# A hybrid decoder step on one core: the mixer in one pass of 576 tokens, and in two token groups with u tiles between the steps of the second

## The chip, the cores and the metric

One Trainium2 chip, one of its cores. The metric is the device time of one execution in microseconds; the kernel was run three times, and one execution more was taken with the hardware profiler.

## The reference

There are 576 tokens of width 1024: 512 of a prompt and 64 of a sample group (8 sequences of 8). Cut to what matters, for both groups:

```python
xn = rms_norm(x, norm1_g)
q, k, v, glu = _project(xn, w_in, q_g, k_g)          # 8 heads of 64, 2 kv heads; glu = val * sigmoid(gate), 512 channels
a = sliding-window attention with sinks (prompt: blocks of 128; sample: cached keys and values, then the new ones)
c = silu(layer_norm(causal depthwise conv of glu, width 31)) @ conv_pw_w
h = x + concat(rms_norm(a), rms_norm(c)) @ w_out
y = h + _peer(rms_norm(h))                            # PEER: 8 heads, top 16 of 128 x 128 experts per token
# _peer: scores of two half-keys, the 16 best of each, the 16 best sums, gate = softmax of those;
#        out = sum over the picks of gelu(u[i] . xn) * gate * v[i], with 16384 experts of width 1024
```

## The kernel before, in words

Five token tiles (`TILES`): tiles 0 to 2 are the 384 dense tokens (`DT`), tile 3 (`TA`, 128 tokens of the prompt) and tile 4 (`TB`, the 64 sample tokens) are the 192 gathered ones (`GT`). Activations lie transposed, channels on the partitions, tokens in the free dimension.

The *mixer* works on all 576 tokens at a time. TensorE multiplies weight blocks out of a ring of four (`wring`, loaded by `load_block` on SP's queue when the block four places earlier has been used) with `xn` (`gemm`, L523): K, four Q, V, then for each of four channel groups the GLU value and gate. Attention goes through eight *units* (token tile, kv head): scores (L589), softmax on VectorE and ScalarE (`softmax_max`, L833, `softmax_div`), transposes (L600), values (L611). There is one buffer of probabilities, so units follow one another. VectorE does the depthwise convolution of three of the four channel groups between the halves of the softmaxes, as chains of 31 dependent taps, each tap one instruction of 512 columns (prompt) and one of 64 (sample) (`conv_taps` at the file's end, L1454; which quarter goes where is `CONV_AT`); TensorE does the fourth with diagonal matrices (L578, L579). Then come the sample's scores, transposes and values (L624 to L643), the means and roots of the norms (`means` L535, `root` L805 on ScalarE, `rstd` L1078 on VectorE), the pointwise product `pw`, the output product in two halves (`woa` of attention, `wob` of convolution), and the second norm (L1223).

*PEER.* The two halves of the experts' work are done in two ways. For the 192 gathered tokens, routing comes first (`key_ranks("a")`, `picks` of TA and TB); then GpSimd gathers for each of 128 picks one row of `u` and one of `v` per token (384 "rows" of 512 KB in all, L1056, ring of 8), and VectorE multiplies or accumulates them (`row`, L1348, L1352). For the 384 dense tokens all 16384 experts are computed: 128 *u tiles* (`dense_u`, L710, 24 matmuls each), each split into a high and a low part by ScalarE (`high`, L915) and VectorE (`low`, L1233), with a Gelu out of PSUM (L941) that SP stores to DRAM; and 128 *v tiles* (L782, 18 matmuls each). Between the two stands the *gate stage*: 64 batches of six tokens, in which VectorE builds two one-hot matrices (`onehots`, L1395), ScalarE scales one (`apply_gates`, L996), TensorE multiplies them (L760), ScalarE copies the result to `Gs` (L1010), all double-buffered, and SP stores it.

The order on every engine is written out by hand, and a few constants say which u tile or row goes where: the u tiles 0 to 16 (`U_TOP` = 17) run beside the picks of TA and TB, 16 beside the ranking of the dense tokens (`key_ranks("b")`), 36 beside their picks, 54 are spread over the 64 gate batches by `u_at` (L62 to L64) and five come after. Of the rows, 66 come before the gate stage, 152 are spread over its batches by `batch_rows` (`V_ROW0`), and the rest over the v tiles by `v_rows`. `EXP_AFTER`, `KEYS_AFTER` and `ROWS_AFTER` name the u tile behind which ScalarE does a piece of the routing. No u tile starts before the keys of the gathered tokens are ranked. In the gate stage TensorE's order is this:

```python
for b in range(NBAT):
    pe.wait_ge(s_ab, 2 * b + 2)      # one-hots of batch b, VectorE
    pe.wait_ge(s_ag, b + 1)          # scaled, ScalarE
    if b >= 2:
        pe.wait_ge(s_gev, b - 1)     # copied out, ScalarE
    # six products, L760
    for n in range(u_at(b), u_at(b + 1)):
        dense_u(n)
```

and ScalarE's is: copy batch b (L1010), scale batch b + 1 (L996), then the Gelu and `high` of the batch's u tiles.

Of the kernel before, what the change touches and what calls it, by code (L numbers as in the profile page):

```python
# [58 lines left out]
U_TOP = 17  # L59
# [13 lines left out]
V_ROW0 = B_ROW0 + 152  # L73
# [13 lines left out]
ROWS_AFTER = {2: TA, 4: TB}  # L87
EXP_AFTER = {5: TA, 13: TB, 39: 0, 51: 1, 63: 2}
KEYS_AFTER = {8: TB, 33: 0, 45: 1, 57: 2}
# [21 lines left out]
BLOCKS += ["woa0", "woa1", "woa2", "pw0", "pw1"] + [f"woa{_m}" for _m in range(3, DC)] + [f"wob{_m}" for _m in range(DC)]  # L111
NMIX = len(BLOCKS)
ROW_WO = BLOCKS.index("woa0") + 2
# [3 lines left out]
def block_row(n):  # L117

    name = BLOCKS[n]
    if name[:2] == "wo":  # L120
        return ROW_WO + int(name[3:])
    if name[:2] == "pw":
        return ROW_WO - 2 + int(name[2:])
    return n if n < NMIX else ROW_WO + DC + (n - NMIX) % NM


def block_use(n):

    name = BLOCKS[n]
    if name[:3] == "val":  # L130
        return f"glu{2 * int(name[3:])}"
    if name[:4] == "gate":
        return f"glu{2 * int(name[4:]) + 1}"
    return {"pw0": "pw1", "pw1": "pw3"}.get(name, name)


CONV_AT = [0, 0, 0, 1, 2, 3, 4, 5, 6, 7, 8, 9, 10, 11, 12, 12, 12]
# [6 lines left out]
def psum_plan():  # L144

    plan = [("ms1", 3), ("K", 0), ("Q0", 1), ("Kn", 3), ("Q1", 2), ("Q0n", 3), ("Q2", 0), ("Q1n", 3), ("Q3", 1),
            ("Q2n", 3), ("V", 2), ("Q3n", 3)]
    for u in range(8):
        plan += [(f"S{u}", 2)] + ([(f"glu{2 * u}", 0)] if u < CC else []) + [(f"PT{u}", 3)]
        plan += ([(f"glu{2 * u + 1}", 1)] if u < CC else []) + [(f"O{u}", 2)]  # L150
    plan += [("taps", 0)]
    plan += [("SS", 2), ("PTS", 3), ("OS", 2), ("msA", 3), ("mean", 0), ("woa0", 2), ("var", 1)]
    plan += [("woa1", 3), ("woa2", 2), ("pw0", 0), ("pw1", 1), ("pw2", 3), ("pw3", 0), ("woa3", 2), ("msC", 1)]
    plan += [("woa4", 3), ("woa5", 0), ("woa6", 2), ("woa7", 3)]
    plan += [(f"wob{m}", m % 3) for m in range(DC)]
    plan += [("ms2", 3)]
# [5 lines left out]
    plan += [(f"xt{TA}", 0), (f"xt{TB}", 0)]  # L162
    for m in range(NM):
        plan += [(f"wqb{m}", m % 2), (f"scb{m}", 2)]
    plan += [(f"tr{t}", t % 2) for t in range(DTI)] + [(f"ht{TA}", 1), (f"ht{TB}", 0)]
    return plan


def hymba_peer(nc, xT_d, wblk_d, cols_d, maskp_d, masks_d, ident_d, ckT_d, cv_d, state_d, keysT_d, u_d, v_d, uT_d,
               gm_d, y_d, pk_d, pv_d, pc_d, sk_d, sv_d, sc_d):  # L170
    use = {}
    uses = [0] * 4
    for name, pair in psum_plan():
        uses[pair] += 1
        use[name] = (pair, uses[pair])

    with ExitStack() as ctx:
# [32 lines left out]
        idx = sb("idx", [P, 2, NPICK], I32)  # L210
        hu = sb("hu", [P, 2, NPICK])
# [3 lines left out]
        with ExitStack() as mixer:  # L215
# [4 lines left out]
            AT = mb("AT", [P, CC, T])  # L220
            cacc = mb("cacc", [P, CC, T])
            qT = mb("qT", [P, CC, T])
            kT = mb("kT", [P, T])
            vtok = mb("vtok", [P, 5, P])
            sq = mb("sq", [P, 2, T])
            Pb = mb("Pb", [P, 1024])
            PTb = mb("PTb", [P, 1024])
            sg = mb("sg", [P, 2, T])
            qS = mb("qS", [P, NDB * GQ * DS])
            maskp = mb("maskp_sb", [P, 2 * WIN])  # L230
            masks = mb("masks_sb", [P, 4, WIN + NS])
            ckT = mb("ckT", [P, NDB, WIN])
            cv = mb("cv", [P, NDB, P])
            gpad = mb("gpad", [P, CC, PAD + SEQ])
            spad = mb("spad", [P, CC, NDB, PAD + DS])
            taps = mb("taps", [P, TAPS, P])
            on1024 = mb("on1024", [P, P])
            on512 = mb("on512", [P, P])
            onblk = mb("onblk", [P, P])
            rs = mb("rs", [P, T])  # L240
            st = mb("st", [P, 8, 8])

        xh = sb("xh", [P, DC, DT], F32R)
        xl = sb("xl", [P, DC, DT], F32R)
        xtok = sb("xtok", [P, 2, D])
# [3 lines left out]
        raw = sb("raw", [P, RAWS, D])  # L249
        hi = sb("hi", [P, 2, D], F32R)  # L250
        lo = sb("lo", [P, 2, D], F32R)
        ring = sb("ring", [P, SLOTS, D])
        gest = sb("gest", [P, 2, 2 * DT])
# [32 lines left out]
        R = [sem(f"psum_ready{i}") for i in range(4)]  # L286
        F = [sem(f"psum_free{i}") for i in range(4)]
# [16 lines left out]
        s_conv_d = sem("conv_by_dve")  # L304
# [61 lines left out]
        def _(sp):  # L366
# [16 lines left out]
            def load_block(n):  # L383
# [3 lines left out]
                if BLOCKS[n][:2] == "wo":  # L387
# [34 lines left out]
            for n in range(NMIX + RING):  # L422
# [10 lines left out]
                if BLOCKS[n] == "woa0":  # L433
                    small_outputs()
                load_block(n)

            sp.wait_ge(s_xn2, DC)
            sp.wait_ge(s_o2, 16 * 15)
            for m in range(NM):
                if m < RAWS:  # L440
                    load_raw(m)
                load_block(NMIX + RING + m)
            for n in range(U_TOP):
                after_u(n)
# [58 lines left out]
        def _(pe):  # L503
            nblk = [0]

            def take(name):
                pair, n = use[name]
                if n > 1:
                    pe.wait_ge(F[pair], n - 1)
                return ps[pair], R[pair]  # L510

# [16 lines left out]

            def means(name, ones, src, n, made):

                out, ready = take(name)
                for k in range(n):
                    pe.wait_ge(made, k + 1)
                    for a in range(2):
                        mm = nc.tensor.matmul(out[:, a * 512:a * 512 + HALF], ones[:, :],  # L535
                                              src(k)[:, a * HALF:(a + 1) * HALF], start=(k == 0), stop=(k == n - 1))
                mm.then_inc(ready, 1)
# [28 lines left out]
            def conv_taps(i):  # L566
# [8 lines left out]
                pair, _ = use["taps"]  # L575
                for j in range(TAPS_AT[i], TAPS_AT[i + 1]):
                    ends = dict(start=(j == 0), stop=(j == TAPS - 1))
                    nc.tensor.matmul(ps[pair][:, 0:SEQ], taps[:, j, :], gpad[:, c, j:j + SEQ], **ends)  # L578
                    mm = nc.tensor.matmul(ps[pair][:, SEQ:T], taps[:, j, :], spad[:, c, :, j:j + DS], **ends)  # L579
                if i == 7:  # L580
                    mm.then_inc(R[pair], 1)

            for u in range(8):
# [8 lines left out]
                if u < CC:  # L592
                    gemm(f"glu{2 * u}", xn)
                else:
                    conv_taps(2 * (u - CC))
# [7 lines left out]
                if u < CC:  # L603
                    gemm(f"glu{2 * u + 1}", xn)
                else:
                    conv_taps(2 * (u - CC) + 1)
# [8 lines left out]

            pe.wait_ge(s_cache, 48)
            out, ready = take("SS")
            for b in range(NDB):
                for g in range(NKV):
                    grp, slot = b // 2, (b % 2) * 2 + g  # L620
                    rows = slice(g * HD, (g + 1) * HD)
                    o = out[slot * 32:slot * 32 + 32, (grp // 2) * 512 + (grp % 2) * 192:]
                    q = qS[rows, b * 32:(b + 1) * 32]
                    nc.tensor.matmul(o[:, 0:WIN], q, ckT[rows, b, :], start=True, stop=True)  # L624
                    mm = nc.tensor.matmul(o[:, WIN:WIN + NS], q, kT[rows, SEQ:T], start=True, stop=True)
            mm.then_inc(ready, 1)
            pe.wait_ge(s_p, 9)
            out, ready = take("PTS")
            for grp in range(4):
# [900 lines left out]
```

## Time and profile before

| | us |
|---|---|
| median of three runs | 1857.13 (1852.23 to 1859.45) |
| profiled execution, own time | 1858.78 |
| its span, first to last instruction | 1857.0 |
| TensorE matmul busy | 1669.9 (90%) |
| VectorE busy | 1433.3 (77%) |
| ScalarE busy | 762.1 (41%) |
| GpSimd busy | 540.2 (29%) |
| mean granted TensorE clock | 0.951 of full |

Busy times overlap between engines, and a busy matmul is not a matmul at its peak, so the shares alone don't name a bound. The kernel has stages with different limits, and the rows below are read by stage. Columns of groups of instructions are: line, engine, operation, what it writes and reads, partitions and elements, count, then busy us, mean ns of one, then the engine's idle time just before them and what ended it.

### The profile page before, as it was taken

The page shows a single profiled execution, that of the slowest core. Times are in us where ns is not written, and L with a number is a line of the kernel's source. Part 1 is how long each engine was busy: PE and PEld are TensorE (multiplying, and loading weights), DVE is VectorE, ACT ScalarE, POOL GpSimd, SP SyncE. Part 2 cuts the span into 40 slices and gives each one's busy share as a digit, 9 for nine tenths or more (in the row PEclk, how much of TensorE's full clock was granted, in tenths as well). Part 3 has the DMA queues.
Part 4 walks back from the last instruction along what each step waited for, and adds up shares of the span by engine and source line. Part 5 has one row for each costly group of instructions (what it writes and reads, how often), then busy time and mean ns, then how long its engine had stood idle before and what let it go on. Part 6 is the DMA issues. An engine that isn't in the chain of part 4 may idle for free.

```text
span 1857.0 us, 23142 instructions
## 1 busy us (share of the span) xinstructions
PE 1669.9 (90%) x8361; PEld 1449.5 (78%) x8361; DVE 1433.3 (77%) x2657; ACT 762.1 (41%) x1274; POOL 540.2 (29%) x395
## 2 busy tenths in 40 slices
PE   7888668989699998999789998999999999999997
PEld 5766446769697777999789898999877877877876
DVE  3466854238777999777899999995978888988876
ACT  3222112112352222444688887884333333333332
POOL 0000000000012333111366566662334433344330
PEclk9998887999799999999899999999999999999999
DMA  6110500125275787777699999999999999999985
GB/s 191 46 46 3 63 1 18 52 77 189 86 255 188 287 276 234 240 230 239 232 393 382 402 385 397 388 381 397 383 343 374 376 349 376 386 375 368 373 316 186
DMA packets 164360, 477.45 MB, mean 257 GB/s; under 512 B 28063, under 2 KB 61535, under 8 KB 162071
## 3 DMA queue, kind: packets, MB, share of 16 engines
q1 hardware_dynamic: 108951, 274.63, 42.6%
q0 software_dynamic: 55296, 201.35, 28.6%
q8 instruction: 67, 1.10, 0.2%
q14 instruction: 46, 0.38, 0.1%
HBM read 420.93 MB, written 54.42 MB: 256 GB/s over the span
## 4 chain that ended last, share of the span: by engine, by line
PE 60%; DVE 29%; issue 5%; ACT 3%; DMA 2%; SPq 0%; DVEq 0%; ACTq 0%
PE ps L782 24%; PE ps L710 17%; PE ps L523 9%; DVE ring L1348 6%; DVE lo L1233 3%; PE ps L760 3%; DVE cacc L1454 2%; DVE gA L1395 2%; DVE tsi L1245 2%; DVE tsi L1248 2%; DVE gB L1395 2%; PE ps L535 2%; DVE sm L1246 2%; DVE acc L1352 2%; DVE tsv L1247 1%
## 5 line engine op out<-in xcount | busy, mean ns | idle before, releaser
L1056 POOL DMA_INDIRECT ring<-in_u,idx x192 | 272.0, 1417 | 909.4 <-DVE ijg L1328 523.9
L1233 DVE TENSOR_TENSOR lo<-raw,hi 128x1024 fp32r<-128x1024 f32 x256 | 313.1, 1223 | 143.8 <-ACT hi L915 141.0
L915 ACT ACTIVATE hi<-raw 128x1024 fp32r<-128x1024 f32 x256 | 270.4, 1056 | 324.3 <-PE ps L782 324.3
L710 PE MATMUL ps<-xh,hi 128*128 128x384 f32 x1024 | 356.9, 349 | 27.2 <-DVE lo L1233 27.2
L1056 POOL DMA_INDIRECT ring<-in_v,idx x192 | 266.7, 1389 | 368.6 <-DVE acc L1352 354.7
L710 PE MATMUL ps<-xl,hi 128*128 128x384 f32 x1024 | 348.5, 340 | 0.0
L710 PE MATMUL ps<-xh,lo 128*128 128x384 f32 x1024 | 347.9, 340 | 0.0
L782 PE MATMUL ps<-hi,ah 128*128 128x512 f32 x768 | 239.9, 394 | 23.0 <-DVE al L1425 22.8
L1352 DVE SCALAR_TENSOR_TENSOR acc<-ring,hu,acc 128x1024 f32<-128x1024 f32 x192 | 245.5, 1279 | 1.6
L782 PE MATMUL ps<-hi,al 128*128 128x512 f32 x768 | 239.7, 394 | 0.0
L782 PE MATMUL ps<-lo,ah 128*128 128x512 f32 x768 | 239.1, 393 | 0.0
L1348 DVE CUSTOM_DVE_ANT_0 ring<-ring,xtok 128x1024 f32<-128x1024 f32 x192 | 226.4, 1218 | 0.3 <-DVE hu L1348 0.3
L710 PEld LDWEIGHTS ps<-xh,hi 128*128 128x128 f32 x1024 | 198.2, 194 | 29.3 <-issue 15.5
L710 PEld LDWEIGHTS ps<-xl,hi 128*128 128x128 f32 x1024 | 197.8, 193 | 0.0
L710 PEld LDWEIGHTS ps<-xh,lo 128*128 128x128 f32 x1024 | 197.0, 192 | 0.0
L782 PEld LDWEIGHTS ps<-hi,ah 128*128 128x128 f32 x768 | 145.5, 190 | 56.6 <-DVE lo L1233 23.5
L782 PEld LDWEIGHTS ps<-hi,al 128*128 128x128 f32 x768 | 146.0, 190 | 30.7
L782 PEld LDWEIGHTS ps<-lo,ah 128*128 128x128 f32 x768 | 145.9, 190 | 30.7
L941 ACT ACTIVATE gest<-ps 128x384 f32<-128x384 f32 x128 | 62.8, 491 | 248.6 <-PE ps L710 237.0
L1010 ACT ACTIVATE Gs<-ps 128x768 f32<-128x768 f32 x64 | 133.5, 2086 | 28.4 <-PE ps L760 28.4
L760 PE MATMUL ps<-gB,gA 128*128 128x128 f32 x768 | 106.1, 292 | 42.7 <-issue 26.3
L680 PE MATMUL ps<-xn,wring 128*128 128x192 f32 (+1 forms) x512 | 133.6, 416 | 5.6 <-DVE xn L1223 5.6
(176 smaller groups left out, 1972.7 us busy)
## 6 DMA issues: line engine op xcount, KB each, us to landing
raw<-in_uT SPq DMA_DIRECT2D x128, 512.0 KB, 5.9
raw<-in_v SPq DMA_DIRECT2D x128, 512.0 KB, 6.2
wring<-in_wblk SPq DMA_DIRECT2D x48, 512.0 KB, 3.5
gelu_matrix<-gest SPq DMA_DIRECT2D x64, 384.0 KB, 7.4
gate_matrix<-Gs SPq DMA_DIRECT2D x16, 1536.0 KB, 8.8
Gl<-gate_matrix SPq DMA_DIRECT2D x128, 192.0 KB, 6.6
gel<-gelu_matrix SPq DMA_DIRECT2D x128, 192.0 KB, 5.7
wring<-in_wblk SPq DMA_DIRECT2D x16, 256.0 KB, 2.5
```

The lines of the kernel that those rows point to most:

```text
L523: mm = nc.tensor.matmul(out[:, a * 512:a * 512 + HALF], w, rhs[:, k, a * HALF:(a + 1) * HALF], start=(k == 0), stop=(k == kc - 1))
L680: mm = nc.tensor.matmul(out[:, 0:w], wring[:, n % RING, k * P:(k + 1) * P], xn[:, k, t0:t0 + w], start=(k == 0), stop=(k == DC - 1))
L710: mm = nc.tensor.matmul(out, a[:, n % 2, w], b[:, c, :], start=(c == 0 and k == 0), stop=(c == DC - 1 and k == 2))
L760: mm = nc.tensor.matmul(ps[b % 2][:, c:c + NKEY], A[:, b % 2, t, :], B[:, b % 2, t, :], start=True, stop=True)
L782: mm = nc.tensor.matmul(ps[t][:, h * 512:(h + 1) * 512], a[:, n % 2, w], b[:, n % 2, h * 512:(h + 1) * 512], start=False, stop=(n == NKEY ...
L915: nc.scalar.activation(hi[:, s % 2, :], raw[:, s % RAWS, :], ACT.Copy).then_inc(s_hi, 1)
L1010: nc.scalar.activation(dst, src, ACT.Copy).then_inc(s_gev, 1)
L1056: pool.indirect_dma_start(ring[:, r % SLOTS, :], None, table, bass.IndirectOffsetOnAxis(idx[:, t, c:c + 1], 0)).then_inc(g_in[r % SLOTS], 16)
L1233: nc.vector.tensor_tensor(lo[:, s % 2, :], raw[:, s % RAWS, :], hi[:, s % 2, :].bitcast(F32), ALU.subtract).then_inc(s_lo, 1)
L1348: nc.vector.tensor_tensor_reduce(got, got, xtok[:, t, :], 1.0, 0.0, ALU.mult, ALU.add, hu[:, t, c:c + 1]).then_inc(g_used, 1)
L1352: nc.vector.scalar_tensor_tensor(out=acc[:, t, :], in0=got, scalar=hu[:, t, c:c + 1], in1=acc[:, t, :], op0=ALU.mult, op1=ALU.add).then_in ...
L1395: nc.vector.tensor_tensor(dst[:, b % 2], iota.unsqueeze(1).broadcast_to([P, BATCH, NKEY]), kT3[:, half, tok:tok + BATCH].unsqueeze(2).broa ...
```

## The change

The attention units and the channel means, norms, pointwise and output products are done for the 384 dense tokens first. The 192 gathered tokens go afterwards, in buffers of their own (`mgb`, `ATb`, `caccb`, `rsb`), with units 6 and 7, the sample's attention and the same chain of norms and products at 192 columns (one full output product `wo` in place of `woa` and `wob`; the pointwise and output blocks are loaded a second time). Between their steps TensorE runs u tiles 0 to 11 (`U_MIX` = 12), with `step` on ScalarE, `low` on VectorE and `after_u` on SP. All later due numbers are raised by 12, so that 42 u tiles are left for the gate batches; `V_ROW0` goes from 152 to 140 rows behind `B_ROW0`. The convolution on VectorE becomes `conv_a` (384 columns, all of it in units 1 to 3) and `conv_b` (128 and 64 columns, 12 quarters from unit 4 to unit 6). PSUM is handed out by banks of 512 columns instead of pairs of banks, and the buffers used only by the late part lie where `xtok`, `acc` and the row ring come later. Q, K, V and the GLU products stay as they are.

```diff
-U_TOP = 17
+U_MIX = 12
+U_TOP = U_MIX + 17
...
-V_ROW0 = B_ROW0 + 152
+V_ROW0 = B_ROW0 + 140
...
-CONV_AT = [0, 0, 0, 1, 2, 3, 4, 5, 6, 7, 8, 9, 10, 11, 12, 12, 12]
+CONV_AT = [0, 0, 0, 2, 4, 6, 8, 10, 12, 12, 12, 12, 12]
...
# SP
+                if BLOCKS[n] == "woa4":
+                    for s in range(RAWS):
+                        load_raw(s)
                 load_block(n)
-            sp.wait_ge(s_xn2, DC)
+            for n in range(8):
+                after_u(n)
...
# TensorE
+            unit_scores(4)
+            unit_scores(5)
+            conv_taps(0)
+            conv_taps(1)
+            unit_transposes(4)
+            conv_taps(2)
+            conv_taps(3)
+            unit_values(4)
+            conv_taps(4)
+            conv_taps(5)
+            unit_transposes(5)
+            conv_taps(6)
+            conv_taps(7)
+            unit_values(5)
...
+            dense_u(0)
+            dense_u(1)
+            unit_transposes(6)
+            unit_scores(7)
+            dense_u(2)
+            unit_values(6)
+            dense_u(3)
+            unit_transposes(7)
+            sample_scores()
+            dense_u(4)
+            unit_values(7)
+            pe.wait_ge(s_conv_b, CC)
+            group_means("meanb", lambda k: caccb[:, k, :], CC)
+            dense_u(5)
+            sample_transposes()
+            dense_u(6)
+            group_means("varb", conv_b, CC, s_sqc, base=CC)
+            sample_values()
+            dense_u(7)
+            group_means("msAb", lambda k: mgb[:, k, :], CC, s_sqa, base=CC)
+            for m in range(CC):
+                group_gemm(f"pwb{m}", ...)
+            dense_u(8)
+            group_means("msCb", conv_b, CC, s_sqcr, base=CC)
+            dense_u(9)
+            for m in range(DC):
+                group_gemm(f"wo{m}", ...)
+                if m >= 2:
+                    square_mean("ms2b", m - 2, DC, DT, GT)
+                if m == 3:
+                    dense_u(10)
+            square_mean("ms2b", DC - 2, DC, DT, GT)
+            dense_u(11)
+            square_mean("ms2b", DC - 1, DC, DT, GT)
...
# VectorE, dense group behind unit 5
+            centred("mean", lambda c: cacc[:, c, :], 0)
+            rstd("msA", rs[:, 0, 0:DT])
+            rstd("var", rs[:, 1, 0:DT])
+            normed(lambda c: cacc[:, c, :], rs[:, 1, 0:DT], 0)
+            merged(lambda c: mg[:, c, 0:DT], lambda c: AT[:, c, :], "ga", rs[:, 0, 0:DT])
+            conv_b(3)
+            conv_b(4)
+            attn_added(0)
+            rstd("msC", rs[:, 1, 0:DT])
+            dve.wait_ge(s_craw, CC)
+            merged(lambda c: mg[:, CC + c, 0:DT], lambda c: AT[:, c, :], "gc", rs[:, 1, 0:DT])
+            for m in range(1, DC):
+                attn_added(m)
+                if m in (3, 5, 7):
+                    conv_b(5 + (m - 3) // 2)
+            for m in range(DC):
+                bank, n = use[f"woa{m}"]
+                dve.wait_ge(F[bank], n)
+                h_added("wob", m, 0, 0, DT)
+                if m in (1, 3, 5):
+                    conv_b(8 + (m - 1) // 2)
+            low(0)
+            low(1)
+            rstd("ms2", rs[:, 0, 0:DT])
+            second_norm(0, 0, DT, rs[:, 0, 0:DT])
+            for c in range(1, DC):
+                second_norm(c, 0, DT, rs[:, 0, 0:DT])
+                x_low(c - 1)
+            x_low(DC - 1)
```

## Rows read from the trace of the kernel before

**Rows 1.** Busy by stage: stretch, length, PE, PEld, DVE, ACT, POOL, PEclk, DMA share, GB/s.
```profile
0.00:409.30 409.30, 329.47 (x1456) 249.51 (x1456) 205.58 (x339) 91.26 (x193) 1.42 (x11) 0.91 0.21 55
409.30:482.80 73.50, 57.24 (x320) 50.92 (x320) 61.99 (x273) 16.02 (x58) 0.00 (x0) 0.87 0.41 137
482.80:892.20 409.40, 392.45 (x2049) 355.81 (x2049) 334.89 (x1029) 153.22 (x199) 88.61 (x74) 0.98 0.71 234
892.20:1262.00 369.80, 329.34 (x2049) 327.20 (x2050) 349.89 (x460) 303.12 (x556) 235.49 (x151) 0.94 0.97 376
...
1293.60:1857.00 563.40, 532.42 (x2304) 437.33 (x2304) 471.50 (x551) 188.72 (x256) 212.22 (x157) 0.98 0.94 351
```

**Rows 2.** Chain that ended last, gate stage: start us, us, what.
```profile
938.53 5.18 PE ps L710 x24
...
989.20 1.34 PE ps L760 x12
990.53 4.17 PE ps L710 x24
```

**Rows 3.** Timeline of ScalarE around batch 6: start us, us, instruction, idle before.
```profile
932.65 2.08 ACT L1010 ACTIVATE Gs<-ps 128x768 f32<-128x768 f32 x1
934.44 1.83 ACT L996 ACTIVATE gA<-gA,kT 128x128 f32<-128x128 f32 x6
938.56 2.09 ACT L1010 ACTIVATE Gs<-ps 128x768 f32<-128x768 f32 x1 [2.29 <-PE ps L760]
...
945.09 2.09 ACT L1010 ACTIVATE Gs<-ps 128x768 f32<-128x768 f32 x1
```

**Rows 4.** Timeline of TensorE, the gate product behind the batch without a tile.
```profile
936.38 2.15 PE L760 MATMUL ps<-gB,gA 128*128 128x128 f32 x12 [3.76 <-issue]
```

**Rows 5.** Timeline of ScalarE, last pair of batches of that kind.
```profile
1226.07 2.08 ACT L1010 ACTIVATE Gs<-ps 128x768 f32<-128x768 f32 x1
...
1238.51 2.08 ACT L1010 ACTIVATE Gs<-ps 128x768 f32<-128x768 f32 x1
```

**Rows 6.** Timeline of ScalarE, batch 19 without a tile.
```profile
1007.09 2.08 ACT L1010 ACTIVATE Gs<-ps 128x768 f32<-128x768 f32 x1
...
1012.43 2.09 ACT L1010 ACTIVATE Gs<-ps 128x768 f32<-128x768 f32 x1 [1.71 <-PE ps L760]
```

**Rows 7.** Groups of VectorE instructions in the v stage, 1300 to 1840 us.
```profile
L1352 DVE SCALAR_TENSOR_TENSOR acc<-ring,hu,acc 128x1024 f32<-128x1024 f32 x162 | 207.0, 1278 | 0.0
L1233 DVE TENSOR_TENSOR lo<-raw,hi 128x1024 fp32r<-128x1024 f32 x126 | 154.1, 1223 | 51.4 <-ACT hi L915 51.4
```

**Rows 8.** Groups of VectorE instructions in the mixer, 0 to 300 us.
```profile
L1454 DVE SCALAR_TENSOR_TENSOR cacc<-gpad,cols_sb,cacc 128x512 f32<-128x512 f32 x90 | 67.6, 751 | 2.9
L1454 DVE SCALAR_TENSOR_TENSOR cacc<-spad,cols_sb,cacc 128x64 f32<-128x64 f32 x90 | 25.1, 279 | 0.0
L1078 DVE RECIPROCAL rs<-rs 128x576 f32<-128x576 f32 x6 | 22.5, 3753 | 49.6 <-ACT rs L805 49.6
```

**Rows 9.** Chain that ended last, units 2 and 3: scores, one pair of taps, scores.
```profile
126.49 2.00 PE ps L589 x8
...
133.46 0.96 DVE cacc L1454 x2
...
182.47 2.00 PE ps L589 x8
```

**Rows 10.** Timeline of TensorE, the prompt's part of taps on diagonal matrices, back to back.
```profile
259.17 1.08 PE L578 MATMUL ps<-gpad,taps 128*128 128x512 f32 x2
```

**Rows 11.** Timeline of TensorE, one query product of 192 columns, 8 chunks.
```profile
418.35 2.87 PE L680 MATMUL ps<-xn,wring 128*128 128x192 f32 x16
```

**Rows 12.** Chain that ended last, two query products of 384 columns, 8 chunks each.
```profile
558.55 10.32 PE ps L680 x32
```

**Rows 13.** Groups of VectorE instructions, 297 to 600 us.
```profile
L1227 DVE TENSOR_TENSOR xl<-xn,xh 128x384 fp32r<-128x384 f32 x8 | 4.5, 558 | 2.9 <-ACT xh L959 1.9
```

**Rows 14.** Timeline of VectorE, copy of the sample's attention.
```profile
295.99 0.42 DVE L1167 COPY AT<-ps 128x256 f32<-128x256 f32 x1 [14.64 <-PE ps L643]
```

More of the change, by code:

```diff
@@ L171, in hymba_peer @@
     use = {}
[L172 to L175, printed above, removed]
+    held = {}
+    after = {}
+    uses = [0] * 8
+    last = [None] * 8
+    for name, *banks in psum_plan():
+        uses[banks[0]] += 1
+        use[name] = (banks[0], uses[banks[0]])
+        held[name] = banks
+        after[name] = [n for n in {last[b]: 0 for b in banks} if n]
+        for b in banks:
+            last[b] = name
     with ExitStack() as ctx:
@@ L527, in gemm, with group_gemm @@
                     nblk[0] += 1
+            def group_gemm(name, src, kc, cut=0, last=True, made=None, base=0):
+                out, ready = take(name)
+                n = nblk[0]
+                if cut == 0:
+                    pe.wait_ge(w_in[n % RING], 16 * (n // RING + 1))
+                for k in range(kc):
+                    if made is not None:
+                        pe.wait_ge(made, base + k + 1)
+                    rhs = src(k)
+                    mm = nc.tensor.matmul(out[:, 0:rhs.shape[1]], wring[:, n % RING, (cut + k) * P:(cut + k + 1) * P],
+                                          rhs, start=(k == 0), stop=(k == kc - 1))
+                mm.then_inc(ready, 1)
+                if last:
+                    nblk[0] += 1
             def means(name, ones, src, n, made):
@@ L536, in means, with group_means @@
                                               src(k)[:, a * HALF:(a + 1) * HALF], start=(k == 0), stop=(k == n - 1))
+                mm.then_inc(ready, 1)
+            def group_means(name, src, n, made=None, base=0):
+                out, ready = take(name)
+                for k in range(n):
+                    if made is not None:
+                        pe.wait_ge(made, base + k + 1)
+                    rhs = src(k)
+                    mm = nc.tensor.matmul(out[:, 0:rhs.shape[1]], on512[:, :], rhs, start=(k == 0), stop=(k == n - 1))
                 mm.then_inc(ready, 1)
@@ L614, in _ @@
                 mm.then_inc(ready, 1)
-            pe.wait_ge(s_cache, 48)
[L617 to L625, printed above, removed]
@@ L712, in dense_u, with sample_scores @@
                 mm.then_inc(s_hud, 1)
+            def sample_scores():
+                out, ready = take("SS")
+                for b in range(NDB):
+                    for g in range(NKV):
+                        grp, slot = b // 2, (b % 2) * 2 + g
+                        rows = slice(g * HD, (g + 1) * HD)
+                        o = out[slot * 32:slot * 32 + 32, (grp // 2) * 512 + (grp % 2) * 192:]
+                        q = qS[rows, b * 32:(b + 1) * 32]
+                        nc.tensor.matmul(o[:, 0:WIN], q, ckT[rows, b, :], start=True, stop=True)
+                        mm = nc.tensor.matmul(o[:, WIN:WIN + NS], q, kT[rows, SEQ:T], start=True, stop=True)
+                mm.then_inc(ready, 1)
@@ L884, in _ @@
-            root("msC")
+                act.sem_inc(F[use[f"PT{u}"][0]], 1)
+            for u in range(CC):
+                unit_exps(u)
+                unit_transposed(u)
+                p = ready(f"glu{2 * u + 1}")
+                if u >= 2:
+                    act.wait_ge(s_glu, 2 * u - 2)
+                nc.scalar.activation(two(sg[:, u % 2, :]), two(p), ACT.Sigmoid).then_inc(s_sig, 1)
+                act.wait_ge(s_sig, u + 1)
+                act.sem_inc(F[use[f"glu{2 * u + 1}"][0]], 1)
```

752 lines of the change are left out of this document (439 added, 313 removed).

## The prediction

> **What bounds the kernel now.** I read the stretches first [rows 1]: mixer to 409.3, the ranking of the gathered tokens to 482.8, u tiles with routing to 892.2, the gate stage to 1262.0 (369.8 us), the v stage from 1293.6 (563.4 us). TensorE is busy throughout, but the change moves work between stages with different limits, so each is read by itself.
>
> In the gate stage VectorE is busy 349.9 of 369.8 us and the DMA engines 97% [rows 1], and one would name either as the bound. The chain of waits in order of time says otherwise: a batch is a gate product of 1.34 us and a u tile of 4.17 us, end to end on TensorE [rows 2], 5.51 us a batch; 64 of those are 352.6 us. Of the 64 batches, `u_at` gives 54 a tile and 10 none. What a batch without a tile costs is the number on which everything hangs. The first such case [rows 3]: ScalarE copies a batch at 932.65, scales the next one's one-hots (934.44, 1.83 us), only then can TensorE multiply (936.38), and the next copy starts at 938.56: 5.91 us, although TensorE had 4.17 us less to do. ScalarE, TensorE, ScalarE stand in series, and the tile filled the hole. Worse, TensorE has paused 3.76 us, the product then takes 2.15 us [rows 4] and the tile behind it 5.18 instead of 4.17 [rows 2]: the granted clock has fallen to its lower level (1.2 GHz), and the next copy comes 6.53 us later [rows 3]. The two batches make 12.44 us where two with tiles make 11.01: the hole costs 1.43. There are nine such pairs behind the first batch. The last makes 12.44 too [rows 5]; six cost 1.43 to 1.46, two 2.2 and 2.3, and one, in which the clock did not fall, has 5.34 us for the empty batch [rows 6] and costs nothing (-0.15). The mean is 1.45. The stage agrees: 352.6 + 10 x 1.45 = 367.1, against 369.8; the 2.7 left are its start and a wait for a store of gelu rows.
>
> **The change, part by part.**
>
> *Gate stage.* The twelve tiles moved ahead come out of it: 42 remain, so 22 batches have none. It also has 140 instead of 152 gathered rows. On VectorE that is 12 x 1.22 + 12 x 1.28 = 30 us less [rows 7], on DMA 12 raw tiles, 12 rows and 6 stores, 15 MB or 40 us at the stage's 376 GB/s, on TensorE 12 x 4.17 = 50 us, and none of them sets the batch. The price is 12 more holes. Bounds of one: -0.17 us (5.34 against 5.51, clock kept, [rows 6]) and 2.3 us (the worst pair); I take the mean of nine, 1.45: +17 us. The holes stay isolated, one or two tiles between them, as now. The granted clock, 0.94 over this stage [rows 1], falls with every hole that pays.
> The Trainium skill (TensorE: Matmul & The Clock Gate, HAM oscillation) says that a matmul kernel with a pause in each step falls to the low level at every one and pays each time. By that rule all 22 pay; at the 1.65 us mean of the eight that paid this would be +22 instead of +17. The trace agrees in eight of nine.
>
> *Mixer, units 0 to 5.* The order of Q, K, V is unchanged. A tap of the convolution covers 512 + 64 columns in the kernel before, 0.96 us a pair [rows 9] and 0.02 for the link. From 751 ns at 512 and 279 ns at 64 [rows 8], 384 columns cost 616 ns and with the link 0.65 us; 128 and 64 columns together 0.58. The dense taps of units 1 to 3 lie 16 ahead of the division instead of 8: 10.2 instead of 7.8 us, which delays the transposes; those behind it stay under the GLU product. A unit lasts 28 us now (126.5 to 182.5 for two, [rows 9]); with +2.4 in each of three, the scores of unit 4 start at 190 instead of 182.5. Units 4 and 5 have 31 taps of 1.08 us on TensorE [rows 10] between their scores, transposes and values (2 us each, [rows 9]), 45.5 us, and the second softmax waits for `conv_b` once, 1.5: 47 us, to 237.
>
> *Dense group to its first u tile.* Every product counts two records a matmul: 16 records of 192 columns take 2.87 us [rows 11], so a block's product costs 2.9 us at 192 columns with 8 chunks. At 384 columns two queries take 10.32 us [rows 12], 0.645 us a matmul, 2.6 us for 4 chunks. On TensorE: four means 10.3, pointwise 10.3, sixteen half products 41.3, squares 5.2, unit 6's scores 2: 69 us. On VectorE: reciprocals fall from 3.75 us [rows 8] to about 2.55 (by columns), four of them 10.2; centring, scaling and two mergings, four each of 0.5 to 0.57 us (a 384-wide one is 0.558, [rows 13]), 8.5; eight quarters of `conv_b`, 62 taps of 0.575, 35.6; sixteen additions 8; two `low` 2.4; the first normed columns 1.1: 66 us. Neither hides the other wholly: the roots and inversions before the pointwise product hold TensorE 5 us, the pointwise product holds VectorE 4, the last addition, square, root and inversion 5. Followed step by step, the first tile starts at 318, 81 us on.
>
> *Gathered group with twelve tiles.* On TensorE: tiles 50.2, five blocks of scores, transposes or values of 2 us each 10, the sample's scores and transposes 2.9, its values 11.2 (of the 14.6 us that VectorE waits for transposes, copy and values together, [rows 14]), four means of 4 matmuls at 0.36 us 5.7, pointwise 5.8, the output product 8 x 2.87 = 23, squares 2.9: 112 us, to 430. Step by step I find 13 us of waiting: 4 before unit 6's transposes, 4 before the output product (ScalarE must finish a tile's Gelu and `high`, then take a root, then VectorE inverts and merges), 5 behind the last tile. That gives 443, and I add 2 for products after pauses at the low clock (bounds 0 and 12): the first query product starts at 445, against 409.3 [rows 1]. The floor, TensorE without a wait behind 237, is 237 + 69 + 112 = 418.
>
> *Ranking of the gathered tokens.* It takes 73.5 us [rows 1], VectorE's. Eight `x_low` of 558 ns [rows 13] leave it, 4.5 us, and the query columns are ready sooner (192 instead of 576 wide, about 2 us). First tile behind it at 445 + 67 = 512, against 482.8: +29 (bounds +2, from the floor, and +42). The twelve tiles in it would be 50 us of TensorE elsewhere, if TensorE set the pace there. From there to the gates the work is the same, with all due numbers raised by 12: 409.4 us.
>
> *V stage.* Twelve rows more: 15.4 us of VectorE. It idles 51.4 us before `low` alone [rows 7], and TensorE's 18 matmuls set a tile; so I take +2 (bounds 0, hidden, and 15, all on the path).
>
> *DMA issues.* Twelve loads of raw tiles and six stores of gelu rows move from the gate stage into the mixer, on SP's queue between the weight blocks. DMA is busy 21% there [rows 1], the blocks of the output product are asked for a tile or more ahead: nothing. Without that cover, a block that lands after its product is due adds its landing, some 3 us, once or twice; that is inside the bounds of the mixer.
>
> Sum: +29 +17 +2 = +48. The profiled execution has a span of 1857.0 us and its own time 1858.78, 1.65 above the median of the three runs (1857.13). So its own time would be 1907 and the median 1905.
>
> **The rivals.**
> *A full resource sets the gate stage.* DMA is busy 97% and VectorE 349.9 of 369.8 us [rows 1]. If DMA sets it, 15 MB fewer take 40 us off, and the tiles moved ahead pay. With the mixer at +22, between its forecast and its floor, that is 1857 + 22 - 40 + 2 = 1841, faster. Against it: batches with a tile repeat in 5.51 us exactly, TensorE's sum, and an empty one isn't shorter. It decides if an empty batch falls under 5 us. Chance 0.10.
> *The waits fill and the holes cost little.* The tiles fill the mixer's waits to +2 or +15, and with more holes the clock falls at half of them: 352.6 + 22 x 0.7 + 2.7 = 371, +1. That gives 1862 to 1875. For it: one hole of nine is free. Chance 0.17.
> *The tiles hold the chain up.* If each of the gathered group's steps waits behind a whole tile and then starts its own root, switch and inversion, the mixer ends 20 us later: 1925. Chance 0.10.
> *Forecast*, chance 0.63: mixer +18 to +40, gates +5 to +22, v stage 0 to +5; 1880 to 1922.
>
> **How the numbers follow.** About 0.5%, 9 us, is what a measurement of this kernel tells from no change. Faster: the first rival and a little more, 0.11. Same: the lower part of the second and the upper of the first, 0.11. Slower: 0.78. The range leaves out most of the first rival and of the third: 1850 to 1922.
>
> **What would show it.** Right: copies of gate batches about 5.9 us apart without a tile and 6.5 behind one, 22 such pairs, the stage near 387 us at a granted clock below 0.94; unit 4's scores near 190, the first u tile near 318, the first query product near 445, tile 12 near 512; VectorE's share in the gate stage well under 0.95. Wrong: a gate stage under 360 us, or copies less than 5.1 us apart; a first query product before 425.

## The result, and the profile after

Slower: 1928.11 us median (1925.14 to 1929.04, four runs) against 1857.04 beside it, a ratio of 1.038 (95% interval 1.036 to 1.041). The profiled execution has a span of 1925.9 us, 68.9 more than before, at a mean granted clock of 0.937 (0.951 before). The direction was forecast, the size was not: 1928 lies above the range's end of 1922.

The same stretches as [rows 1], of the kernel after, bounded by the same events (first query product, first u tile behind the ranking, first gate product, transposes, v tiles). The columns are those of [rows 1]; the fifth stretch, the last five u tiles, is 31.4 us, and 31.6 before:

```profile
0.00:444.60 444.60, 380.42 (x1744) 293.39 (x1744) 249.70 (x489) 138.27 (x273) 1.42 (x11) 0.92 0.30 84
444.60:513.30 68.70, 55.82 (x320) 51.10 (x320) 55.29 (x265) 12.21 (x48) 0.00 (x0) 0.90 0.40 123
513.30:921.90 408.60, 392.15 (x2049) 355.45 (x2049) 334.76 (x1029) 153.40 (x198) 88.65 (x74) 0.98 0.72 236
921.90:1315.00 393.10, 308.28 (x1762) 304.64 (x1763) 325.33 (x436) 287.12 (x532) 203.16 (x140) 0.86 0.89 321
1315.00:1346.40 31.40, 28.85 (x184) 28.53 (x182) 8.43 (x9) 9.69 (x14) 0.93 (x1) 0.99 0.96 345
1346.40:1925.90 579.50, 536.65 (x2304) 440.44 (x2304) 485.09 (x563) 188.53 (x256) 239.00 (x169) 0.97 0.94 351
```

Against [rows 1]: the mixer takes 35.3 us more and the ranking 4.8 less, the middle stage 0.8 less, the gate stage 23.3 more, the v stage 16.1 more; that makes 69. In the gate stage every engine has less to do than before, DMA is down from 97% to 89%, and it is longer all the same, with the clock down from 0.94 to 0.86.

The marks of the mixer, from the chain that ended last (start, us, what):

```profile
191.84 2.96 PE ps L653 x16
...
233.92 1.89 PE ps L677 x16
...
444.66 7.12 PE ps L748 x32
...
514.67 15.23 PE ps L780 x72
```

Unit 4's scores start at 191.8 (forecast 190), unit 5's values end at 235.8 (237), the first query product starts at 444.7 (445), tile 12 at 514.7 (512). The first u tile starts at 320.8 (318).

One pair of batches in the gate stage, ScalarE's timeline, to be held beside [rows 3]:

```profile
995.36 2.08 ACT L1217 ACTIVATE Gs<-ps 128x768 f32<-128x768 f32 x1
997.16 1.83 ACT L1203 ACTIVATE gA<-gA,kT 128x128 f32<-128x128 f32 x6
1002.02 2.09 ACT L1217 ACTIVATE Gs<-ps 128x768 f32<-128x768 f32 x1 [3.04 <-PE ps L906]
...
1008.85 2.08 ACT L1217 ACTIVATE Gs<-ps 128x768 f32<-128x768 f32 x1
```

and TensorE in the chain of waits over the same batches, beside [rows 2, 4]:

```profile
989.82 4.17 PE ps L780 x24
...
999.09 2.90 PE ps L906 x12
1001.99 5.49 PE ps L780 x24
1007.48 1.34 PE ps L906 x12
```

The empty batch takes 6.66 us, the one behind it 6.83. The pause of TensorE is 3.77 us (3.76 before), but the product behind it takes 2.90 in place of 2.15, the tile 5.49 in place of 5.18. Over the stage, 22 batches without a tile take 6.50 us in the mean (before: ten, 6.12), 22 behind them 6.33 (6.44), the other 19 5.50 (5.53).

The v stage, what waited for what between 1363 and 1893 us (total, times, longest):

```profile
DVE mt L1739 <- issue: 39.7, 7, 6.7
...
PEld ps L928 <- DVE lo L1476: 35.3, 8, 6.2
PE ps L928 <- DVE al L1747: 32.0, 7, 5.8
```

In the kernel before the same three are 28.7, 23.5 and 20.2 us, at seven, eight and seven places. The seven places are the boundaries between groups of 16 v tiles. VectorE's timeline and SP's at the first of them:

```profile
1408.01 1.28 DVE L1677 SCALAR_TENSOR_TENSOR acc<-ring,hu,acc 128x1024 f32<-128x1024 f32 x1
1413.88 0.56 DVE L1739 TENSOR_TENSOR mt<-gel,Gl 128x384 f32<-128x384 f32 x1 [4.59 <-issue]
```
```profile
1404.87 0.43 SPq L441 DMA_DIRECT2D Gl<-gate_matrix  x1
```

SP asks for the last of the 16 gate blocks of the next group when VectorE has done `mt` of the last tile of the old one. The next `mt` needs it, so a whole landing lies on the path: 9.0 us from 1404.87 to 1413.88. How long a landing is depends on the load. The median for a gate block (1400 to 1840 us) is 7.6 us here and 6.7 before. The DMA engines' throughput in that window of the kernel after, in 40 slices of 11 us:

```profile
GB/s 400 291 375 356 394 401 400 324 313 361 404 401 400 400 298 379 402 398 400 401 280 320 324 400 400 401 399 239 386 352 394 400 400 326 330 360 370 400 399 399
```

They mostly run near 400 GB/s, and the deepest drops come every sixth to seventh slice, at the boundaries, where the stage itself waits. A share of 94% (0.94 in the last stretch above, as in [rows 1]) is such a pattern: full, with gaps.

### The profile page after: what moved, and what is told of

Read it like the earlier page. It is cut to its first block, busy times and chain, and to the rows that moved or that the text cites. A ratio compares the mean times of both kernels' runs of the same rounds, so it can differ in the third digit from the quotient of the medians.

```text
span 1925.9 us, 23368 instructions
## 1 busy us (share of the span) xinstructions
PE 1702.2 (88%) x8361; PEld 1473.5 (77%) x8361; DVE 1458.6 (76%) x2787; ACT 789.2 (41%) x1320; POOL 533.2 (28%) x395
## 4 chain that ended last, share of the span: by engine, by line
PE 65%; DVE 24%; issue 7%; ACT 3%; DMA 1%; SPq 0%; DVEq 0%; ACTq 0%
PE ps L928 23%; PE ps L780 22%; PE ps L906 5%; PE ps L560 4%; DVE ring L1673 4%; PE ps L576 3%; DVE lo L1476 2%; DVE tsi L1573 2%; DVE tsi L1570 2%; DVE sm L1571 2%; DVE cacc L1334 1%; DVE gA L1717 1%; DVE tsv L1572 1%; DVE caccb L1353 1%; DVE acc L1677 1%
## 5 line engine op out<-in xcount | busy, mean ns | idle before, releaser
L1263 POOL DMA_INDIRECT ring<-in_u,idx x192 | 259.7, 1352 | 993.5 <-DVE ijg L1653 554.2
L780 PE MATMUL ps<-xh,hi 128*128 128x384 f32 x1024 | 366.1, 358 | 31.8 <-DVE lo L1476 26.3
L1263 POOL DMA_INDIRECT ring<-in_v,idx x192 | 272.1, 1417 | 361.2 <-DVE acc L1677 338.5
L780 PE MATMUL ps<-xl,hi 128*128 128x384 f32 x1024 | 354.6, 346 | 0.0
L780 PE MATMUL ps<-xh,lo 128*128 128x384 f32 x1024 | 353.5, 345 | 0.0
L780 PEld LDWEIGHTS ps<-xh,hi 128*128 128x128 f32 x1024 | 204.3, 199 | 37.1 <-DVE lo L1476 28.8
L780 PEld LDWEIGHTS ps<-xl,hi 128*128 128x128 f32 x1024 | 203.8, 199 | 0.0
L780 PEld LDWEIGHTS ps<-xh,lo 128*128 128x128 f32 x1024 | 201.7, 197 | 0.0
L906 PE MATMUL ps<-gB,gA 128*128 128x128 f32 x768 | 124.6, 325 | 87.0 <-issue 63.9
L928 PEld LDWEIGHTS ps<-hi,ah 128*128 128x128 f32 x768 | 146.4, 192 | 68.4 <-DVE lo L1476 35.3
L906 PEld LDWEIGHTS ps<-gB,gA 128*128 128x128 f32 x768 | 117.6, 234 | 90.9 <-issue 75.2
```

Of the source, the lines that this page charges most:

```text
L780: mm = nc.tensor.matmul(out, a[:, n % 2, w], b[:, c, :], start=(c == 0 and k == 0), stop=(c == DC - 1 and k == 2))
L906: mm = nc.tensor.matmul(ps[b % 2][:, c:c + NKEY], A[:, b % 2, t, :], B[:, b % 2, t, :], start=True, stop=True)
L928: mm = nc.tensor.matmul(ps[t][:, h * 512:(h + 1) * 512], a[:, n % 2, w], b[:, n % 2, h * 512:(h + 1) * 512], start=False, stop=(n == NKEY ...
L1263: pool.indirect_dma_start(ring[:, r % SLOTS, :], None, table, bass.IndirectOffsetOnAxis(idx[:, t, c:c + 1], 0)).then_inc(g_in[r % SLOTS], 16)
```

## The experiments

Each was run in three rounds beside the kernel before, with a profile of its own. "Before" and "after" name the two kernels; differences of stages are between profiled executions. The gate stage is measured here from the first gate product to the first transpose behind the stage: 370.4 us before, 393.6 after.

**Twelve rows back into the gate stage.**

```diff
 # after
-V_ROW0 = B_ROW0 + 140
+V_ROW0 = B_ROW0 + 152
```

> The changed kernel with 152 instead of 140 gathered rows in the gate stage, so 12 fewer in the v stage. If the serial chain of ScalarE and TensorE sets a gate batch, the rows are free there: gate stage 393 us as in the changed kernel (within 4), v stage back from 579.5 to about 564, total 1913. If VectorE or DMA sets the gate stage, the 12 rows cost it what they save later: gate stage +15, total 1926 to 1930.

Measured: 1909.66 us (1903.66 to 1915.21), ratio 1.028 (1.023 to 1.032). The v stage falls from 579.4 to 556.1 us, the gate stage goes from 393.6 to 391.0: these twelve gathered rows are free in the gate stage, as the reading "the chain of ScalarE and TensorE sets it" wants, and in the v stage they are not.

**The same shift of rows alone.**

```diff
 # before
-V_ROW0 = B_ROW0 + 152
+V_ROW0 = B_ROW0 + 140
```

> The kernel before with 140 instead of 152 rows in the gate stage, nothing else. Chain theory: gate stage stays at 370 us (within 3), v stage grows by about 15, total 1872. Resource theory: gate stage shrinks by 12 rows of 1.28 us, 15, and the total stays at 1857, or falls if the v stage has room for them.

Measured: 1875.04 us (1871.87 to 1878.22), ratio 1.008 (1.005 to 1.010). The v stage is 578.9 us, 15.5 more, the gate stage 373.3 in place of 370.4: twelve rows fewer there win nothing. What the change adds to the v stage is the moved rows and nothing else of it.

**Twelve holes more and nothing else.** Twelve u tiles leave the gate batches for the end, behind the stage.

```diff
 # before
-U_TAIL = NKEY - 5
+U_TAIL = NKEY - 17
```

> The kernel before with 12 u tiles taken out of the gate stage and put behind it (17 instead of 5 tiles in the tail), the mixer untouched. Chain theory: 12 more batches without a tile cost 1.5 to 1.8 us each, the gate stage grows by 18 to 22 us although it has 50 us less of TensorE work, the tail by 12 x 4.17 = 50: total 1925 to 1930. Resource theory: the gate stage shrinks by 12 x 1.22 us of VectorE or more, the total is 1857 + 50 - 15 = 1892 or less.

Measured: 1935.22 us (1928.67 to 1938.9), ratio 1.041 (1.037 to 1.046). The windows of gate stage, the 17 tiles with the transposes, and v stage:

```profile
895.00:1287.30 392.30, 309.48 (x1776) 305.86 (x1777) 337.96 (x446) 285.90 (x526) 224.81 (x152) 0.86 0.92 339
1287.30:1366.30 79.00, 76.45 (x458) 75.96 (x456) 23.13 (x21) 26.36 (x37) 0.94 (x1) 1.00 0.75 238
1366.30:1926.90 560.60, 531.05 (x2304) 436.13 (x2304) 471.55 (x551) 188.71 (x256) 217.88 (x157) 0.98 0.94 352
```

The twelve tiles cost their full 50 us where they went, and taking them out made the gate stage 22 us longer, not shorter. The rival of a full resource falls: DMA went from 97% to 92% and it got slower.

**Holes kept, clock kept.** Dummy matmuls fill TensorE's pause in each empty batch.

```diff
 # after, TensorE's gate loop
+                if u_at(b) == u_at(b + 1):
+                    for i in range(13):
+                        nc.tensor.matmul(ps[2][:, 0:P], hT[:, i % DC, 0:P], ident[:, :], start=True, stop=True, ...)
```

> The changed kernel with 13 matmuls of 128 columns into an unused PSUM bank (about 2.9 us) in each of the 22 gate batches without a tile. Clock theory: TensorE's pause falls from 3.8 to under 1 us, the granted clock stays up, an empty batch takes 5.34 us and the next 5.51, so each pair falls from 12.83 to 10.85 us and the total by 22 x 2 = 43, to 1885; granted clock of the stage from 0.86 to 0.97 or more. If the empty batches are long because of waits for VectorE or ScalarE alone, nothing changes, 1928, or it gets longer by the added matmuls.

Measured: 1889.22 us (1886.37 to 1892.41), ratio 1.016 (1.012 to 1.019). ScalarE's copies around the same empty batch, and the stage:

```profile
988.88 2.08 ACT L1221 ACTIVATE Gs<-ps 128x768 f32<-128x768 f32 x1
...
994.23 2.09 ACT L1221 ACTIVATE Gs<-ps 128x768 f32<-128x768 f32 x1 [1.71 <-PE ps L906]
...
999.73 2.08 ACT L1221 ACTIVATE Gs<-ps 128x768 f32<-128x768 f32 x1
```
```profile
925.90:1279.90 354.00, 333.47 (x2348) 329.92 (x2349) 322.87 (x434) 285.86 (x526) 208.83 (x140) 0.99 0.95 357
```

The clock is 0.99 and the stage 354.0 us in place of 393.6. An empty batch takes 5.35 us, one behind it 5.50, nearly throughout. So the price of the 22 holes, 39.6 us, is that of the granted clock. The series ScalarE, TensorE, ScalarE by itself would take 0.16 us less than a batch with a tile.

**Holes filled with half tiles.** `dense_u` takes a range of chunks; a tile behind an empty batch runs its first four chunks there.

```diff
 # after; the same in before
                 for n in range(u_at(b), u_at(b + 1)):
-                    dense_u(n)
+                    dense_u(n, DC // 2 if b and u_at(b - 1) == u_at(b) else 0)
+                if u_at(b) == u_at(b + 1):
+                    dense_u(u_at(b), 0, DC // 2)
...
```

> The kernel after with the u tile behind each batch that had none split in two on TensorE: the products of its first four chunks run in the batch without a tile, those of its last four in its own. Nothing else moves. If the gate stage of the kernel after is set by the fixed chain of an empty batch (5.9 to 6.5 us whatever TensorE has to do) and by the clock behind it, the 22 pairs fall from 12.8 us to about 11 and the stage from 393 to 345 to 355 us: about 1885. If a full DMA or the gate chain itself set the stage, nothing is won: 1920 or more.

Measured: 1886.49 us (1883.71 to 1888.16), ratio 1.014 (1.011 to 1.017); gate stage 348.7 us, nearly all batches between 5.33 and 5.53.

```profile
927.00:1275.70 348.70, 276.09 (x1777) 263.10 (x1778) 322.10 (x434) 285.36 (x526) 216.25 (x140) 0.99 0.96 362
```

> The kernel before with the same edit in its ten empty batches. Holes theory: 10 holes at 1.3 us each go, 369.8 becomes 355 to 360, with VectorE's 349.9 us next in line: about 1848. If DMA (97% busy there) sets the stage: within 3 us of the kernel before.

Measured: 1844.09 us (1839.07 to 1845.15), ratio 0.991 (0.988 to 0.994); gate stage 354.4 us in place of 370.4, DMA 100% busy at 394 GB/s. Ten holes gave 16 us back, 22 gave 45. With the holes gone in both, the change is still 42 us slower (1886.5 against 1844.1).

**Is it VectorE's time in the v stage?** The rows there are accumulated over 936 of 1024 columns.

```diff
 # after, row(r)
+                    w = 936 if r >= V_ROW0 else D
-                    ...(out=acc[:, t, :], in0=got, ..., in1=acc[:, t, :], ...)
+                    ...(out=acc[:, t, 0:w], in0=got[:, 0:w], ..., in1=acc[:, t, 0:w], ...)
```

> The kernel after, in which the rows of the v stage (behind V_ROW0) are accumulated over 936 of 1024 columns; the last 88 columns of the gathered tokens lack those terms. That takes about 0.11 us from each of 175 accumulations, 18 us of VectorE, and leaves every transfer, queue and wait as it is. If the v stage's additional 16 us are VectorE's time (its instructions as such, or gates that are turned into products late because VectorE has more before them), the v stage falls from 579 to 560 to 565 us, about 1911. If they are the DMA's load (12 more gathered rows beside the same loads, gates landing 0.7 us later), it stays at 575 or more, 1923 or more.

Measured: 1924.88 us (1924.14 to 1930.14), ratio 1.037 (1.034 to 1.039). VectorE has 16 us less and the stage stays (578.8 us; 579.5 in the kernel after):

```profile
1349.40:1928.20 578.80, 538.19 (x2304) 442.01 (x2304) 468.68 (x563) 188.55 (x256) 237.40 (x169) 0.97 0.94 352
```

**Is it the transfers?** The same bytes as twelve rows, taken from the loads of the v tiles.

```diff
 # after, load_raw(s)
-                sp.dma_start(raw[:, s % RAWS, :], src)...
+                w = D if s < NKEY else 928
+                sp.dma_start(raw[:, s % RAWS, 0:w], src[:, 0:w])...
```

> The kernel after, whose v tiles are loaded by 928 of their 1024 columns (the last 96 hold older values, so that part of the dense tokens' output is another). Every instruction, queue entry and wait stays, VectorE's time too; 128 x 48 KB = 6.3 MB fewer are moved in the v stage, as much as twelve gathered rows of 512 KB carry. In the run with 936 columns accumulated VectorE had 15 us less and the v stage stayed at 578.8 us. If the 16 us that the change added to the v stage are its transfers (the DMA engines 98% busy, near 400 GB/s between the group boundaries), the stage falls from 579.4 to 560 to 566 us: 1909 to 1915. If they are neither VectorE nor DMA but the order of the queues, it stays at 575 or more: 1923 or more.

Measured: 1918.39 us (1911.3 to 1926.67), ratio 1.033 (1.028 to 1.038); these four runs scatter more than those of the kernel after, as do those of the kernel before beside them (1853.62 to 1868.45), and the profiled one is the lowest.

```profile
1347.50:1909.30 561.80, 529.20 (x2304) 435.11 (x2304) 484.65 (x563) 188.56 (x256) 243.78 (x169) 0.99 0.95 352
```

VectorE works 485 us as in the kernel after and the stage is 17.6 us shorter. 6.3 MB at the stage's 352 GB/s are 17.9 us. The waits at the boundaries shrink with it, from 39.7 us (39.3 with 936 columns) to 29.6:

```profile
DVE mt L1740 <- issue: 29.6, 7, 4.7
```

One profile could be chance, but the others say how much a v stage scatters. From its first matmul to the end it takes 576.4 to 581.6 us in the six profiled kernels with `V_ROW0` at 140 rows and all bytes moved, and 556.1 to 563.4 in the four with 152 (all ten ask for one gate block per tile). This one, 561.9, has 140 rows and the bytes of 152, and falls among the latter. So in this profile the bytes alone carry the v stage's loss. The median of the runs fell by 10 us rather than 17.6, and the longest of the four (1926.67) lies among those of the kernel after, so how much of it each execution gives back is less sure.

**Gates two blocks per tile.** The next group's 16 blocks are asked for in eight tiles, so that none is asked for at the boundary.

```diff
 # after; the same in before (SP, v stage)
-                if n // JG + 1 < NG:
-                    load_gates(n // JG + 1, n % JG)
+                if n // JG + 1 < NG and n % JG < JG // 2:
+                    load_gates(n // JG + 1, 2 * (n % JG))
+                    load_gates(n // JG + 1, 2 * (n % JG) + 1)
```

> The kernel after with the gate blocks of the next group of 16 v tiles loaded two per tile in the first eight tiles of a group, where it loads one per tile over all sixteen. In the kernel after, each of the seven group boundaries begins with a wait for the last gate block and an issue gap of 4.5 to 6.7 us in the chain, and VectorE stands for the gates' transposed copies 39.7 us in all. Theory 1, the v stage's extra 16 us are gates that land later because the stage has more row traffic beside them: the boundary stalls go, 25 to 30 us with them, and what the change cost in the v stage goes as well; about 1900. Theory 2, the extra 16 us are VectorE's twelve additional row accumulations (15.4 us) in a stage whose tiles are paced by VectorE or TensorE whatever the gates do: the boundary stalls are given back in later tiles, no more than 5 us are won, 1923 or more.

Measured: 1905.04 us (1903.65 to 1907.43), ratio 1.024 (1.022 to 1.027).

> The kernel before with the same edit. Theory 1: its seven boundaries have gaps of 3.1 to 5.6 us and 28.7 us of VectorE's standing; 15 to 20 us are won, about 1840, so that the distance between the two kernels shrinks by the 10 us that the change added there. Theory 2: within 5 us of 1857 to 1862.

Measured: 1845.94 us (1843.55 to 1847.94), ratio 0.992 (0.989 to 0.995). The v stages of the two, after's first:

```profile
1347.30:1902.90 555.60, 531.68 (x2304) 430.91 (x2304) 485.45 (x563) 188.26 (x256) 234.68 (x169) 0.99 0.98 366
```
```profile
1296.80:1846.10 549.30, 529.56 (x2304) 431.60 (x2304) 471.72 (x551) 188.28 (x256) 211.65 (x157) 0.99 0.97 360
```

The stalls at the boundaries are gone, 24 and 14 us with them, and twelve rows now cost 6.3 us in place of 16. Where the rows' bytes bite, then, is the landing that lies on the path seven times: no stall, and the stage absorbs most of them.

**How much of the twelve tiles hides in the mixer?**

```diff
 # after, dense_u(n)
+                last = 0 if n < U_MIX else DC - 1
-                for c in range(DC):
+                for c in range(last + 1):
...
-                        pe.wait_ge(s_xl, c + 1)
+                        pe.wait_ge(s_xl, DC)
...
```

> The kernel after, in which each of the twelve u tiles of the mixer has 3 matmuls in place of 24, so that seven eighths of those tiles' sums are left out; their loads, splits, Gelus and stores stay. TensorE's load between unit 6 and the queries falls by 12 x 3.65 = 44 us. My working of the mixer has TensorE as its bound there (112 us of 125, 13 of waiting): the first query product then comes 30 to 44 us before 444.7, at 400 to 415, and the time is 1885 to 1900. If the chain of norms on ScalarE and VectorE sets the pace and the tiles only fill its waits, it comes at 430 or later, 1914 or more.

Measured: 1905.71 us (1904.57 to 1913.9), ratio 1.028 (1.024 to 1.031). TensorE's timeline:

```profile
424.18 7.12 PE L748 MATMUL ps<-xn,wring 128*128 128x192 f32 x32 [4.86 <-DVE xn L1466]
```

The first query product comes 20.5 us earlier, between the two expectations. Tile 0 gives nothing: with the edit it waits for all of `xl` and starts at 327.6 instead of 320.8, and in the kernel after it was held by the same `xl` and ended at 328.1. The other eleven tiles were 40 us shorter, so about 20 us of them had been lying in waits of the chain of softmaxes, norms and roots: TensorE is the bound of the gathered group only while the tiles are there. So the tiles cost about half their time in the mixer. What the regrouping adds on top is not paid for: with nearly no tiles, the mixer still ends at 424 in place of 409.

**The two repairs together, and with rows moved.**

> The kernel before with both of the edits that won time: u tiles split over the ten empty batches (15 us alone) and gates loaded two per tile (14 us alone). They lie in different stages, so they add: 1829. If the second needs DMA room that the first takes, or the other way round: 1840.

Measured: 1832.49 us (1827.5 to 1835.12), ratio 0.986 (0.983 to 0.990). The two savings nearly add: 24 us against the kernel before, where 15 and 13 were measured alone, each beside the kernel before of its own rounds. The kernel before with both repairs is faster than either kernel without them.

> As the run before it, with V_ROW0 at 140 instead of 152 rows behind B_ROW0. With the holes filled VectorE sets the gate stage (354 us in the run with the split alone, VectorE 350), so twelve rows less take 5 to 10 us from it; with the early gates twelve rows more cost the v stage 6 us (555.6 against 549.3) instead of 16. Sum about 0: 1825 to 1832. If rows cost the v stage 16 us as without the early gates: 1840.

Measured: 1836.1 us (1834.48 to 1837.47), ratio 0.989 (0.986 to 0.992). The v stage is 6.5 us longer, as forecast; the gate stage stays at 356.2 us to the tenth. I had put VectorE as its limit, and VectorE with 15 us less changes nothing there. No batch of any profiled run takes less than 5.32 us, about the 5.35 of the series ScalarE, TensorE, ScalarE, and most batches with a whole tile take 5.51 as they did.

> The kernel before with split tiles and early gates (1832.5) and four more rows beside the picks of each dense token tile (ROWS_PICK 10 in place of 6), so that twelve rows leave the v stage for the stage of u tiles and routing, where the DMA engines are 71% and VectorE 82% busy. DMA as the v stage's bound: 6.3 MB fewer there, 549.9 falls by 6 (what twelve rows cost between the two kernels with early gates) to 16 us, the middle stage stays: 1817 to 1827. If VectorE's picks can't take 12 x 1.28 us more without holding TensorE up, the middle stage grows by up to 15 us and nothing is won: 1832 or more.

Measured: 1835.77 us (1835.46 to 1837.07), ratio 0.987 (0.983 to 0.992). The v stage falls from 549.9 to 536.6 us, and the first gate product comes at 910.7 in place of 894.4: what DMA gains, VectorE's picks lose, 12 x 1.28 us in full and a little more. With 12 rows fewer the v stage is 13 us shorter even with early gates, more than the 6 us that twelve more cost; the two directions differ, and no run says why.

## Why the prediction was wrong

The error is 23 us. 14 of it are one term, the v stage, and 6 another, the price of a hole.

*V stage, +2 forecast, +16 measured.* The step that failed: "It idles 51.4 us before `low` alone [rows 7], and TensorE's 18 matmuls set a tile; so I take +2 (bounds 0, hidden, and 15, all on the path)". I costed the rows in VectorE's time and looked for cover there. A row is also 512 KB. At the 351 GB/s of the stage [rows 1] twelve are 6.3 MB and 17.9 us, a term that the prediction had worked out for the gate stage and left out where the DMA engines were nearly as busy. Less VectorE time left the stage as it was, fewer bytes shortened it. Where the bytes bite was not in the working either: the seven waits for a gate block grew by 11 us, from 28.7 to 39.7, and without these waits the rows cost 6.3 us. The bound from above, 15 us, was wrong for the same reason.

*Gate stage, +17 forecast, +23.3 measured.* The mechanism was right but for one part, named below: no resource sets the batch, a hole costs, the clock falls behind it, and twelve more holes alone made the stage 22 us longer. The size was off: a pair costs 1.82 us (12.83, the mean of 22, against 2 x 5.50), or 1.78 without the first, where the mean of nine without the first was 1.45 in the trace before. The product behind a pause shows it. It takes 2.29 us in the mean of the nine before, between 1.58 and 2.90, and 2.73 in the mean of 21 after, 2.90 in twelve of them, the longest that any gate product of the two kernels takes (1.58 where the clock has stayed up). None of the pauses was free; before, one of nine was. So a mean over nine did not carry over to 22 in another spacing; why more of them fall wholly in the low level stays open. The Trainium skill (TensorE: Matmul & The Clock Gate, HAM oscillation) has a kernel with a pause in every step pay at every one; by that rule I had given +22, and here the trace agrees with it better than with my mean. It is not strict, though: with twelve rows put back, one of the 22 pauses was free again (an empty batch of 5.33 us, the pair 10.86). My reason for the hole, ScalarE, TensorE and ScalarE in series, was wrong as a cost: with the clock kept such a batch takes 5.35 us, less than 5.51. The price is the clock's.

*Mixer and ranking, +29 forecast, +30.5 measured.* Right by its steps, each mark within 3 us. TensorE is idle 12 of 127 us between 318 and 445 (13 were counted). What the sum did not say is that the chain stands close behind: of 40 us taken out of the tiles, 20 were not given back. The middle stage and the last five u tiles, forecast as unchanged, were 1 us shorter together.

*DMA issues, nothing.* Right: the middle of the mixer shows no late block.

The rest of the error is 2 us: this execution's span lies 2.2 us below the median of its runs, where before's lay 0.1 below its own.

*The rivals.* The full resource (1841) is refuted by the run with twelve more holes. "The waits fill and the holes cost little" named one thing that exists, half the tiles hide, but that half is in the forecast's sum too, and the holes did cost. The tiles holding the chain up by 20 us did not occur: the first query product was due at 445 and came at 444.7. The answer above the range came from none of them. With the v stage at its measured 16 us the forecast would have been 1919, still inside; the 6 us that the holes cost more than forecast put the answer over the end, at 1925, and the small terms make it 1928.

## What to carry to other kernels

Cost a moved piece of work on every resource that it uses, its bytes first where a stage's transfer rate is flat at its ceiling with gaps. A wait for a block that was only just asked for turns load on the DMA engines into time, again at every boundary; asking earlier gave 23 us here, and moving twelve rows back 18. When tiles are taken out of a stage that they keep TensorE awake in, spread the rest thinner (half a tile in each step) instead of leaving steps empty: that repair alone gave 42 us to this kernel and 15 to the one before.

## What the runs showed of the hardware

Twelve pauses of 3.76 us more cost 22 us, though TensorE had 50 us less to do: a pair of batches around a pause takes 12.83 us, and 10.85 when 13 dummy matmuls of 128 columns fill the pause. Work that computes nothing won 39 us of the kernel's time.

The DMA engines reach 394 GB/s at a share of 100% in the gate stage of the split kernel before, and about 400 GB/s between boundaries in the v stage. A gate block's landing lengthened from 6.7 to 7.6 us in the median with twelve gathered rows more beside it.

With the rows returned, the kernel after has a v stage of 556.1 us, 7 less than the kernel before with the same rows in the same places. 6 of the 7 lie in the waits for gate blocks (22.8 us against 28.7); no run explains why they are shorter.
